# Loading and multiplying the gate and up matrices of two neighbouring experts together, in 64-row groups

## The chip, the cores and the metric

The kernel runs on one NeuronCore of a Trainium2 chip. The metric is the device time of one execution in microseconds (us); lower is better. All tensors are float32.

## The reference, cut to what matters

Two layers are computed on 256 tokens of width 1024. Each layer has an attention mixer (MLA, block-sparse and dilated heads in parallel) and then a mixture of experts. The change touches the experts alone:

```python
# 64 experts in 8 groups, top-2 inside the best group, D_MODEL 1024, D_EXPERT 256
def one_block(args):
    toks, e = args
    xb = x_pad[toks]                                  # the tokens of expert e
    hb = jax.nn.silu(xb @ w1[e]) * (xb @ w3[e])       # gate and up: 1024 -> 256 each
    return hb @ w2[e]                                 # down: 256 -> 1024
x = layer_norm(ALPHA * x + ffn, ln2_g[l], ln2_b[l])
```

Every expert has tokens or may have them, so all 64 experts' weights are read in each layer: w1 and w3 of 1 MB each and w2 of 1 MB per expert, 192 MB per layer.

## The kernel before, in words

**Tiling.** The program is written out by hand for each engine, with semaphores. Of each layer, an attention part comes first (lines 793 to 919 on TensorE), then the experts. These are taken four at a time: a batch is 4 experts (`NB`) with 32 token slots each (`BLK`), so 128 slots, and there are 16 batches per layer (`BATCHES`). The loop bound `m` is read from `iters` and is 14 here. Batches 0 and 1 are written out, 2 to 13 run in a loop of two batches (`Fori(2, m, 2)`, one on the even and one on the odd buffers), 14 is written out, and 15 has a form of its own (`last_batch`, lines 1174 to 1218) in which weights come in smaller parts.

**One batch on TensorE** (`batch`, lines 1154 to 1172), in this order: `up_gate` for the 4 experts (line 1030): for each expert 8 chunks c of the contraction, each a product of a 128-row, 32-column stationary piece of `xg` with 512 moving columns (gate and up side by side), the chunks spread over the four 32-column groups of the array. The partial sums of the four column groups are copied to `partial` (DVE for experts 0 and 2, line 1626; ACT for 1 and 3, line 1897 through the helper at 1724) and added by `fold` (1065). `turn_gated` (1071) transposes the slot weights. `gather(b + 1)` (1015) makes the next batch's `xg` in banks 2 and 3: 8 chunks of 128 slots, each summed over two token tiles, with a column piece of `x` stationary and the 0/1 matrix `chosen` moving. DVE (1569) and ACT (1880) copy the two banks to `xg`, 4 chunks of 128x128 each, and apply the norm's scale and shift, which stand per partition in `g_cols`. `turn_hidden_pairs` (1086) turns the hidden values; DVE copies them (1646). TensorE waits for both halves of the next `xg` (lines 1167, 1168), since `down_pairs` (1100) writes banks 2 and 3. DVE (1662) and ACT copy its result, and `add_all` (1112) adds it to the output banks.

**down_pairs already works on pairs.** The w2 matrices of two experts come in one transfer with 16 KB per partition (`load_w2_pairs`, line 397): partitions 0 to 63 hold expert 2q, 64 to 127 hold expert 2q+1. A product takes 64 rows and 32 columns of the array. Expert k writes column group k and reads row half k % 2, so each column group sees one row half only:

```python
q, z = k // 2, k % 2
rows = slice(64 * z, 64 * z + 64)
last = mm(bank[2 + h][BLK * k:BLK * (k + 1), :], hT_pair[rows, c, BLK * q:BLK * (q + 1)],
          w2_pairs[parity][q][rows, c, 512 * h:512 * h + 512], start=c == 0, stop=c == 3)
```

**Transfers.** All weights go through SyncE's queue. In a batch, w1 and w3 of expert k are two transfers of 1 MB (8 KB per partition, line 389), issued when the batch two earlier has used the slot (`part_psum`, line 486), and the two w2 pairs (2 MB each) when its down products are done (`y2_psum`). There are two sets of buffers, even and odd. The loads of batches 0 and 1 are issued during attention.

Of the kernel before, what the change touches and what calls it, by code (L numbers as in the profile page):

```python
# [19 lines left out]
P = 128  # L20
NT = SEQ // P
# [7 lines left out]
DC = DM // P  # L29
NE, NG, EPG, FE, TOP_K = 64, 8, 8, 256, 2  # L30
BLK = 32
# [49 lines left out]
def program(nc, a, consts, const_at, out):  # L81
# [12 lines left out]
    w2 = a["moe_w2"].rearrange("l e (p c) d -> (l e) p (c d)", c=2)  # L94
    w2_pair = a["moe_w2"].rearrange("l (g z) (p c) d -> (l g) (z p) (c d)", z=2, c=4)
# [4 lines left out]
    with ctx:  # L100
# [6 lines left out]
        small = sb("small", 416)  # L107
# [17 lines left out]

        w2_pairs = [pair_views(w2_even), pair_views(w2_mem)]
        w13_slots = [w13_views(w13_even), w13_views(w13_mem)]
# [67 lines left out]
        xg = part(DC * P).rearrange("p (c s) -> p c s", c=DC)  # L195
# [53 lines left out]
        n2_cols = small[:, 400:416].rearrange("p (v c) -> p v c", v=2)  # L249
        shift = small[:, 76:78]  # L250
# [20 lines left out]
        cols_in = Signal("norm_columns_in", 6 * 16)  # L271
# [95 lines left out]
        def _(sp):  # L367
# [3 lines left out]
            for l in range(DEPTH):  # L371
# [109 lines left out]
                def load_first(j, back, e, parity, last=False, by_matrix=False):  # L481
                    for k in range(NB):
# [3 lines left out]
                        sp.wait_ge(part_psum.sem, (b0 + j) * NB + (part_psum.start + k + 1 - back))  # L486
                        plain(sp)
                        load_w13(e, k, parity, last, (1,) if by_matrix and k == 0 else (0, 1))

                def load_batch(j, back, e, parity, last=False):  # L490
                    load_first(j, back, e, parity, last)
                    sp.wait_ge(y2_psum.sem, (b0 + j) + (y2_psum.start + 1 - back // NB))
                    plain(sp)
# [36 lines left out]
        def _(pool):  # L530
# [5 lines left out]
            for l in range(DEPTH):  # L536
# [9 lines left out]
                after(pool, l, cols_in, 96)  # L546
# [39 lines left out]
        def _(pe):  # L586
# [15 lines left out]
            xc = x.rearrange("p t (c d) -> p t c d", c=DC)  # L602
            slots_of = [ident.rearrange("p (q z s) -> p z q s", q=2, z=2)[:, z] for z in range(2)]
            for l in range(DEPTH):
# [415 lines left out]
                def up_gate(j, parity, k):  # L1020
                    b = b0 + (j + parity)
                    pe.wait_ge(w13_in[parity][k].sem, (b0 + j) * 16 + (32 - 16 * l * (parity and k == NB - 1)))
# [11 lines left out]
                def first_up_gate():  # L1034
                    pe.wait_ge(w13_in[0][0].sem, b0 * 16 + 32)
# [94 lines left out]
                def first_batch():  # L1130
                    first_up_gate()
                    up_gate(0, 0, 1)
                    after(pe, l, seed_act, 1)
                    seed_rows(0)
                    up_gate(0, 0, 2)
                    up_gate(0, 0, 3)
# [17 lines left out]
                def batch(j, parity, pairs=True):  # L1154
                    b = b0 + (j + parity)
                    pe.wait_ge(xg_dve.sem, b + 1)
                    for k in range(NB):
                        up_gate(j, parity, k)
# [815 lines left out]
```

## Time and profile before

| what | us |
|---|---|
| median of 3 runs | 1159.87 (1158.64 to 1160.63) |
| the profiled execution's own time | 1159.31 |
| its span, first to last instruction | 1157.5 |
| TensorE busy | 1040.3 (90%) |
| VectorE (DVE) busy | 384.4 (33%) |
| ScalarE (ACT) busy | 236.8 (20%) |
| HBM read | 439.07 MB, 380 GB/s over the span |
| mean granted TensorE clock | 0.991 |

Times in the profile count from the first instruction. TensorE's busy time is the time in which at least one product runs; products on different groups of the array overlap, so the mean duration of one product is longer than its share of the busy time. "Idle before, releaser" is the time an engine stood still ahead of an instruction, and what ended that.

### The profile page before, as it was taken

Reading aid. Unit: us, or ns where it says so; the run is one execution under the profiler, and the core shown is the slowest. Engines: PE = TensorE matmul, PEld = TensorE weight load, DVE = VectorE, ACT = ScalarE, POOL = GpSimd, SP = SyncE. Lnnn points to the kernel's source line nnn. Section 1 sums busy time; section 2 is a strip of 40 time slices with the busy share of each in tenths; the row PEclk is TensorE's granted clock in tenths of the full one; section 3 lists DMA queues with packets and bytes.
Section 4 is the critical chain, followed back from the end, with each engine's and each line's share of the span. In section 5 each row is a group of like instructions: output and inputs, shape, how many; then the busy total and the mean of one; then the engine's idle time right before and its main releaser. Section 6 shows DMA issues by size and latency. Waiting matters only on the chain.

```text
span 1157.5 us, 19198 instructions
## 1 busy us (share of the span) xinstructions
PE 1040.3 (90%) x7546; PEld 519.1 (45%) x7546; DVE 384.4 (33%) x1093; ACT 236.8 (20%) x587; POOL 18.7 (2%) x36
## 2 busy tenths in 40 slices
PE   9999988888989988887999999989988989888888
PEld 6665753334433333333456657434433333333333
DVE  4875532222222222121268656222222222221213
ACT  1245321111111111111122543111111111111111
POOL 0010000000000000000000100000000000000000
PEclk9999999999999999999999999999999999998999
DMA  9957699999999999999995676999999999999997
GB/s 309 348 222 291 258 390 416 422 420 423 423 424 422 424 423 423 423 422 422 386 323 217 267 298 273 412 410 421 422 422 422 424 422 423 421 423 423 422 422 275
DMA packets 86029, 440.75 MB, mean 381 GB/s; under 512 B 17376, under 2 KB 36960, under 8 KB 44512
## 3 DMA queue, kind: packets, MB, share of 16 engines
q1 hardware_dynamic: 85696, 439.50, 93.9%
q8 instruction: 29, 0.48, 0.2%
q0 software_dynamic: 144, 0.58, 0.1%
q14 instruction: 16, 0.13, 0.0%
q10 hardware_dynamic: 144, 0.07, 0.0%
HBM read 439.07 MB, written 1.05 MB: 380 GB/s over the span
## 4 chain that ended last, share of the span: by engine, by line
PE 54%; SPq 32%; DMA 4%; DVE 4%; issue 3%; ACT 2%; POOL 0%; DVEq 0%; POOLq 0%
SPq L389 24%; PE bank L1030 9%; PE bank L662 9%; PE bank L1100 7%; SPq L399 7%; PE bank L1112 5%; PE bank L1015 5%; PE bank L788 4%; DMA w_even<-in_moe_w 3%; PE bank L1106 2%; PE bank L652 2%; DMA w_odd<-in_moe_w 2%; PE bank L1065 1%; PE bank L922 1%; SPq L514 1%
## 5 line engine op out<-in xcount | busy, mean ns | idle before, releaser
L1724 ACT ACTIVATE moe<-bank 128x512 f32<-128x512 f32 (+2 forms) x164 | 84.1, 523 | 596.6 <-PE bank L1030 337.5
L1112 PE MATMUL bank<-moe 128*128 128x512 f32 (+1 forms) x264 | 119.3, 593 | 23.7 <-DVE moe L1662 22.5
L1626 DVE COPY moe<-bank 128x512 f32<-128x512 f32 x64 | 44.2, 691 | 250.0 <-PE bank L1030 245.4
L1030 PE MATMUL bank<-w_even,moe 128*32 128x512 f32 x992 | 115.5, 610 | 11.5 <-DMA w_even<-in_moe_w 11.5
L1100 PE MATMUL bank<-w_even,moe 64*32 64x512 f32 x896 | 99.0, 590 | 18.3 <-ACT moe L1880 16.7
L1015 PE MATMUL bank<-moe,x 128*128 128x128 f32 x960 | 113.3, 277 | 1.9 <-DVE moe L1662 1.9
L1030 PE MATMUL bank<-w_odd,moe 128*32 128x512 f32 x992 | 110.6, 594 | 4.0 <-DMA w_odd<-in_moe_w 4.0
L1015 PEld LDWEIGHTS bank<-moe,x 128*128 128x128 f32 x960 | 110.6, 193 | 2.2 <-issue 2.2
L1100 PE MATMUL bank<-w_odd,moe 64*32 64x512 f32 x768 | 84.8, 590 | 15.7 <-DVE moe L1646 9.0
L1662 DVE COPY moe<-bank 128x512 f32<-128x512 f32 x32 | 22.1, 691 | 219.6 <-PE bank L1100 194.5
L1112 PEld LDWEIGHTS bank<-moe 128*128 128x128 f32 x264 | 47.2, 189 | 96.1 <-DVE moe L1662 49.0
L662 PE MATMUL bank<-w_even,w_odd 128*128 128x384 f32 x240 | 81.3, 489 | 0.0
L1030 PEld LDWEIGHTS bank<-w_even,moe 128*32 128x32 f32 x992 | 30.9, 111 | 88.6 <-issue 67.6
L1030 PEld LDWEIGHTS bank<-w_odd,moe 128*32 128x32 f32 x992 | 30.1, 110 | 82.2 <-issue 69.3
L1100 PEld LDWEIGHTS bank<-w_even,moe 64*32 64x32 f32 x896 | 32.8, 107 | 73.7 <-issue 73.7
L1880 ACT ACTIVATE moe<-bank,small 128x128 f32<-128x128 f32 x120 | 45.1, 456 | 98.5 <-PE bank L1015 98.5
L662 PEld LDWEIGHTS bank<-w_even,w_odd 128*128 128x128 f32 x240 | 44.5, 190 | 29.1 <-issue 2.0
L1065 PE MATMUL bank<-moe,constants 128*32 128x512 f32 (+1 forms) x272 | 35.4, 589 | 23.8 <-ACT moe L1724 23.8
L1100 PEld LDWEIGHTS bank<-w_odd,moe 64*32 64x32 f32 x768 | 28.1, 107 | 63.2 <-issue 63.2
L1634 DVE SCALAR_TENSOR_TENSOR moe<-moe,bank 128x256 f32<-128x256 f32 x32 | 13.5, 421 | 126.8 <-ACT moe L1900 126.8
L1569 DVE TENSOR_SCALAR moe<-bank,small 128x128 f32<-128x128 f32 x120 | 41.0, 403 | 24.6 <-PE bank L1015 24.6
L788 PE MATMUL bank<-w_odd 128*128 128x512 f32 x96 | 44.9, 602 | 0.1
(195 smaller groups left out, 904.7 us busy)
## 6 DMA issues: line engine op xcount, KB each, us to landing
w_odd<-in_moe_w SPq DMA_DIRECT2D x140, 1024.0 KB, 30.3
w_even<-in_moe_w SPq DMA_DIRECT2D x136, 1024.0 KB, 28.6
w_even<-in_moe_w SPq DMA_DIRECT2D x28, 2048.0 KB, 29.1
w_odd<-in_moe_w SPq DMA_DIRECT2D x24, 2048.0 KB, 30.3
w_even<-in_w_in SPq DMA_DIRECT2D x24, 768.0 KB, 11.6
w_odd<-in_w_out SPq DMA_DIRECT2D x4, 2048.0 KB, 13.4
w_odd<-in_moe_w SPq DMA_DIRECT2D x8, 512.0 KB, 12.3
w_even<-in_w_in SPq DMA_DIRECT2D x4, 416.0 KB, 6.8
```

Of the source, the lines that this page charges most:

```text
L389: sp.dma_start(w13_slots[parity][k][:, m, :, :].rearrange("p c f -> p (c f)"), (w1, w3)[m][l * NE + e * NB + k]).then_inc(sig.sem, 16)
L399: sp.dma_start(w2_pairs[parity][q].rearrange("p c d -> p (c d)"), w2_pair[l * (NE // 2) + e * (NB // 2) + q]).then_inc(w2_in[parity][2 * q ...
L662: last = mm(to[:, 0:GW], rows[:, c, :], weights[:, c, :], start=fresh and c == 0, stop=c == DC // 2 - 1, skip_group_check=True)
L788: last = mm(mix_bank[t][h][:, :], oT[:, c, t * P:(t + 1) * P], w_out_half[h][:, c, :], start=c == 0, stop=c == DC - 1, skip_group_check=True)
L1015: last = mm(bank[2 + c // 4][:, c % 4 * P:(c % 4 + 1) * P], xc[:, t, c, :], chosen[:, t, :], start=t == 0, stop=t == 1)
L1030: last = mm(bank[k % 2][BLK * q:BLK * (q + 1), :], xg[:, c, BLK * k:BLK * (k + 1)], w[:, :, c, :], start=c < 4, stop=c >= 4)
L1065: last = mm(to[BLK * k:BLK * (k + 1), 0:cols.stop - cols.start], const("fold"), partial[:, k, cols], start=True, stop=True)
L1100: last = mm(bank[2 + h][BLK * k:BLK * (k + 1), :], hT_pair[rows, c, BLK * q:BLK * (q + 1)], w2_pairs[parity][q][rows, c, 512 * h:512 * h + ...
L1112: return mm(Y[t][h][:, lo - 512 * h:hi - 512 * h], scatter[:, t * P:(t + 1) * P], y_rows[:, lo:hi], start=False, stop=True, skip_group_che ...
L1626: nc.vector.tensor_copy(partial[:, k, :], bank[2 if first and k == 0 else 0][:, :]).then_inc(part_dve.sem, 1)
L1724: return fn(dst, src, ACT.Copy)
L1880: last = fn(xg[:, c, :], bank[3][:, (c - 4) * P:(c - 3) * P], ACT.Identity, scale=g_cols[:, 0, c:c + 1], bias=g_cols[:, 1, c:c + 1])
```

## The change

Batches 3 to 14 of each layer take w1 and w3 in pairs of experts. Batches 0, 1, 2 and 15 keep the old form. Per batch, SyncE issues 4 transfers of 2 MB (16 KB per partition) in place of 8 of 1 MB, and both of a pair wait until both experts of the slot pair are used. `up_gate_pair` computes with 64-row, 32-column pieces: 16 chunks per expert, experts 2q and 2q+1 alternating on row halves 0 and 1, each in its own bank (0 to 3), chunk c on column group c % 4. `gather_pairs` makes the matching `xg`: for each of 16 chunks it writes 64 slots of expert 2q to partitions 0 to 63 and 64 of expert 2q+1 to 64 to 127. DVE and ACT copy 8 pieces of 128x64 each with `pair_cols`, which four more small transfers per layer bring. The even loop now runs from 4 on, and batches 2 and 3 are written out ahead of it.

```diff
+    w1_pair = a["moe_w1"].rearrange("l (g z) (p c) f -> (l g) (z p) (c f)", z=2, c=2 * DC)
+    w3_pair = a["moe_w3"].rearrange("l (g z) (p c) f -> (l g) (z p) (c f)", z=2, c=2 * DC)
...
+        xg_pair = xg_mem.rearrange("p (c s) -> p c s", c=2 * DC)
...
+                    for z in range(2):
+                        sp.dma_start(pair_cols[64 * z:64 * z + 64, v, :], a[name].rearrange("l (p c) -> l p c", c=2 * DC)[l]
+                                     ).then_inc(cols_in.sem, 16)
...
-                        sp.wait_ge(part_psum.sem, (b0 + j) * NB + (part_psum.start + k + 1 - back))
+                        done = 2 * (k // 2) + 2 if last else k + 1
+                        sp.wait_ge(part_psum.sem, (b0 + j) * NB + (part_psum.start + done - back))
...
+                def load_pairs(j, back, e, parity):
+                    for q in range(NB // 2):
+                        sp.wait_ge(part_psum.sem, (b0 + j) * NB + (part_psum.start + 2 * q + 2 - back))
+                        plain(sp)
+                        for m_ in range(2):
+                            sp.dma_start(w13_pairs[parity][q][:, m_, :, :].rearrange("p c f -> p (c f)"),
+                                         (w1_pair, w3_pair)[m_][l * (NE // 2) + e * (NB // 2) + q]
+                                         ).then_inc(w13_in[parity][2 * q + m_].sem, 16)
...
+            xc_pair = x.rearrange("p t (c d h) -> p t h c d", c=DC, h=2)
+            chosen_pair = chosen.rearrange("p t (q z s) -> p t z q s", q=2, z=2)
...
+                def gather_pairs(b):
+
+                    pe.wait_ge(chosen_ok.sem, b + 1)
+                    plain(pe)
+                    for h in range(2):
+                        for c in range(DC):
+                            for t in range(NT):
+                                for z in range(2):
+                                    last = mm(bank[2 + h][64 * z:64 * z + 64, 64 * c:64 * c + 64], xc_pair[:, t, h, c, :],
+                                              chosen_pair[:, t, z], start=t == 0, stop=t == 1)
+                        last.then_inc(gathered[h].sem, 1)
+
+                def up_gate_pair(j, parity, q):
...
+                    for c in range(2 * DC):
...
+                        i = c % 4
+                        for z in range(2):
+                            rows = slice(64 * z, 64 * z + 64)
+                            last = mm(bank[2 * q + z][BLK * i:BLK * (i + 1), :], xg_pair[rows, c, BLK * q:BLK * (q + 1)],
+                                      w[rows, :, c, :], start=c < 4, stop=c >= 2 * DC - 4)
+                            if c == 2 * DC - 1:
+                                last.then_inc(part_psum.sem, 1)
...
-                with pe.Fori(2, m, 2) as j:
+                batch(0, 1, 32 + 32 * l, pairs=False, next_pairs=False)
+                batch(2, 0, 48 + 32 * l)
+                batch(2, 1)
+                with pe.Fori(4, m, 2) as j:
                     batch(j, 0)
                     batch(j, 1)
-                batch(m, 0)
+                batch(m, 0, next_pairs=False)
...
+                    if pairs:
+                        for c in range(DC):
+                            last = ts(xg_pair[:, c, :], bank[2][:, 64 * c:64 * c + 64], pair_cols[:, 0, c:c + 1],
+                                      pair_cols[:, 1, c:c + 1], ALU.mult, ALU.add)
+                        last.then_inc(xg_dve.sem, 1)
+                        return
...
-                        nc.vector.tensor_copy(partial[:, k, :], bank[2 if first and k == 0 else 0][:, :]).then_inc(part_dve.sem, 1)
+                        source = bank[k if w13_pairs else 2 if first and k == 0 else 0]
+                        nc.vector.tensor_copy(partial[:, k, :], source[:, :]).then_inc(part_dve.sem, 1)
...
+                    if pairs:
+                        for c in range(DC):
+                            last = fn(xg_pair[:, DC + c, :], bank[3][:, 64 * c:64 * c + 64], ACT.Identity,
+                                      scale=pair_cols[:, 0, DC + c:DC + c + 1], bias=pair_cols[:, 1, DC + c:DC + c + 1])
+                        last.then_inc(xg_act.sem, 1)
+                        return
```

The third and fourth partial sums of a batch are now read from banks 2 and 3, so the waits of `up_gate` for a free bank (line 1025) fall away in these batches. The waits on `w13_in` count one increment per transfer of a pair.

## Rows read from the trace of the kernel before

**Rows 1.** The page: GB/s in 40 equal slices of the span.

```profile
GB/s 309 348 222 291 258 390 416 422 420 423 423 424 422 424 423 423 423 422 422 386 323 217 267 298 273 412 410 421 422 422 422 424 422 423 421 423 423 422 422 275
```

**Rows 2.** The page: the chain that ended last, by engine (SPq is SyncE's queue).

```profile
PE 54%; SPq 32%; DMA 4%; DVE 4%; issue 3%; ACT 2%; POOL 0%; DVEq 0%; POOLq 0%
```

**Rows 3.** Timeline of TensorE, batch 8 of layer 0: start us, us, what, count [idle before].

```profile
357.85 7.07 PE L1030 MATMUL bank<-w_even,moe 128*32 128x512 f32 x64
...
367.00 3.74 PE L1015 MATMUL bank<-moe,x 128*128 128x128 f32 x32
370.67 0.69 PE L1086 MATMUL bank<-constants,moe 128*64 128x64 f32 x16
372.63 7.07 PE L1100 MATMUL bank<-w_even,moe 64*32 64x512 f32 x64 [1.28 <-ACT moe L1880]
```

**Rows 4.** Timeline of TensorE: first up_gate products of batches 3, 11, 15, both layers.

```profile
226.84 3.64 PE L1030 MATMUL bank<-w_odd,moe 128*32 128x512 f32 x32
...
436.56 5.36 PE L1030 MATMUL bank<-w_odd,moe 128*32 128x512 f32 x48
...
553.58 5.40 PE L1030 MATMUL bank<-w_odd,moe 128*32 128x512 f32 x48
...
799.54 7.07 PE L1030 MATMUL bank<-w_odd,moe 128*32 128x512 f32 x64
...
1009.35 5.36 PE L1030 MATMUL bank<-w_odd,moe 128*32 128x512 f32 x48
...
1127.41 5.36 PE L1030 MATMUL bank<-w_odd,moe 128*32 128x512 f32 x48
```

**Rows 5.** Timeline of TensorE: stretches that ran at the lower clock, both layers.

```profile
472.68 3.49 PE L1030 MATMUL bank<-w_even,moe 128*32 128x512 f32 x16 [2.86 <-DMA w_even<-in_moe_w]
...
1045.31 2.69 PE L1030 MATMUL bank<-w_even,moe 128*32 128x512 f32 x16 [2.87 <-DMA w_even<-in_moe_w]
...
1051.13 4.71 PE L1015 MATMUL bank<-moe,x 128*128 128x128 f32 x32
...
1104.82 3.36 PE L1030 MATMUL bank<-w_even,moe 128*32 128x512 f32 x16 [2.87 <-DMA w_even<-in_moe_w]
```

**Rows 6.** DMA view: 295 to 300 us (16 KB packets), then 305 to 319 us (8 KB).

```profile
DMA packets 147, 2.15 MB, mean 429 GB/s; under 512 B 16, under 2 KB 16, under 8 KB 16
...
DMA packets 812, 5.89 MB, mean 421 GB/s; under 512 B 93, under 2 KB 93, under 8 KB 93
```

**Rows 7.** Timeline of SyncE's queue, layer 0: w1 and w3 of batches 2 and 3 issued.

```profile
149.72 8.99 SPq L389 DMA_DIRECT2D w_even<-in_moe_w  x8
...
179.88 5.96 SPq L389 DMA_DIRECT2D w_odd<-in_moe_w  x8
```

**Rows 8.** Timeline of TensorE: four 32-row groups at once, each with its bank.

```profile
66.31 0.71 PE L735 MATMUL bank<-w_odd 32*128 32x256 f32 x8
```

**Rows 9.** Timeline of TensorE, 370.70 to 371.10 us: 14 of the 16 products.

```profile
370.67 0.63 PE L1086 MATMUL bank<-constants,moe 128*64 128x64 f32 x14
```

**Rows 10.** Groups of ACT by form, whole span: busy us, mean ns | idle before.

```profile
L1724 ACT ACTIVATE moe<-bank 128x512 f32<-128x512 f32 x92 | 54.9, 597 | 556.4 <-PE bank L1030 337.5 <-PE bank L1100 195.2 <-PE bank L947 15.8
L1880 ACT ACTIVATE moe<-bank,small 128x128 f32<-128x128 f32 x120 | 45.1, 456 | 98.5 <-PE bank L1015 98.5
...
L1724 ACT ACTIVATE moe<-bank 128x256 f32<-128x256 f32 x40 | 15.3, 383 | 26.5 <-PE bank L1106 20.0 <-PE bank L1059 3.4 <-PE bank L1071 3.2
...
L1852 ACT ACTIVATE moe<-moe 128x64 f32<-128x64 f32 x4 | 1.0, 257 | 10.9 <-DVE moe L1506 10.9
```

**Rows 11.** Timelines of ACT and DVE, batch 8 of layer 0: the copies of the next xg.

```profile
370.78 1.50 ACT L1880 ACTIVATE moe<-bank,small 128x128 f32<-128x128 f32 x4 [3.19 <-PE bank L1015]
...
368.99 1.37 DVE L1569 TENSOR_SCALAR moe<-bank,small 128x128 f32<-128x128 f32 x4 [0.67 <-PE bank L1015]
371.40 0.42 DVE L1646 COPY moe<-bank 128x256 f32<-128x256 f32 x1 [1.04 <-PE bank L1086]
```

**Rows 12.** DMA view, 250 to 540 us: the queue that carries instructions.

```profile
q14 instruction: 2, 0.02, 0.0%
```

More of the change, by code:

```diff
@@ L124, in pair_views, with w13_pair_views @@
             return [mem[:, q * 2 * W2:(q + 1) * 2 * W2].rearrange("p (c d) -> p c d", c=4) for q in range(NB // 2)]
+        def w13_pair_views(mem):
+            return [mem[:, q * 2 * W13:(q + 1) * 2 * W13].rearrange("p (m c f) -> p m c f", m=2, c=2 * DC)
+                    for q in range(NB // 2)]
         w2_pairs = [pair_views(w2_even), pair_views(w2_mem)]
+        w13_pairs = [w13_pair_views(w13_even), w13_pair_views(w13_mem)]
         w13_slots = [w13_views(w13_even), w13_views(w13_mem)]
@@ L545, in _ @@
                 after(pool, l, router_in, 32)
-                after(pool, l, cols_in, 96)
+                after(pool, l, cols_in, 160)
                 after(pool, l, comb, 8)
@@ L1152, in first_batch, with batch @@
                     add_all()
-                def batch(j, parity, pairs=True):
+                def batch(j, parity, seen=None, pairs=True, next_pairs=True):
                     b = b0 + (j + parity)
                     pe.wait_ge(xg_dve.sem, b + 1)
-                    for k in range(NB):
-                        up_gate(j, parity, k)
+                    if seen is None:
+                        for q in range(NB // 2):
+                            up_gate_pair(j, parity, q)
+                    else:
+                        for k in range(NB):
+                            up_gate(j, parity, k, seen)
                     pe.wait_ge(part_dve.sem, b * 2 + 2)
@@ L1163, in batch @@
                     turn_gated(bank[1])
-                    gather(b + 1)
+                    (gather_pairs if next_pairs else gather)(b + 1)
                     pe.wait_ge(scT_sb.sem, b + 1)
@@ L1601, in _ @@
                 weigh_scores(1)
-                after(v, l, cols_in, 96)
+                after(v, l, cols_in, 160)
                 def scale_first(c):
@@ L1613, in _, with batch @@
                 m, b0 = start_batches(v, base, l)
-                def batch(j, last_of_all, e_next, first=False, pairs=False):
+                def batch(j, last_of_all, e_next, first=False, pairs=False, w13_pairs=False, next_pairs=False):
                     b = b0 + j
@@ L1893, in _, with copy_partial @@
                 scale_first(7).then_inc(xg_act.sem, 1)
-                def copy_partial(b, k):
+                def copy_partial(b, k, source=bank[1]):
                     act.wait_ge(part_psum.sem, b * NB + (part_psum.start + k + 1))
-                    copy(partial[:, k, :], bank[k % 2][:, :]).then_inc(part_act.sem, 1)
+                    copy(partial[:, k, :], source[:, :]).then_inc(part_act.sem, 1)
                 def squash():
@@ L1904, in copy_scatter, with batch @@
                     copy(scatter, source[:, 0:SEQ]).then_inc(scT_sb.sem, 1)
-                def batch(j, first=False):
+                def batch(j, first=False, w13_pairs=False, next_pairs=False):
                     b = b0 + j
                     copy_partial(b, 1)
-                    copy_partial(b, 3)
+                    copy_partial(b, 3, bank[3 if w13_pairs else 1])
                     act.wait_ge(gu_psum.sem, b + 1)
@@ L1940, in _ @@
                 batch(0, first=True)
-                with act.Fori(1, m) as j:
-                    batch(j)
-                batch(m)
+                batch(1)
+                batch(2, next_pairs=True)
+                with act.Fori(3, m) as j:
+                    batch(j, w13_pairs=True, next_pairs=True)
+                batch(m, w13_pairs=True)
                 last_batch(m + 1)
```

56 lines of the change are left out of this document (35 added, 21 removed).

## The prediction, made before the changed kernel was built or run

> **What bounds the kernel now.** I read the GB/s line of the page first. In the two long expert stages it stands at 420 to 424 in slice after slice [rows 1]: the transfers never pause there, so each layer's experts last as long as their weights take to arrive. The chain that ended last says so too: a third of it is SyncE's queue, which only issues loads [rows 2]. The third view is TensorE's timeline, and it is the one that decides here, since TensorE is close behind. The reader is to see in it the order of one batch [rows 3] and the pace of batches [rows 4]. From the first up_gate product of batch 3 to that of batch 11, eight batches take 436.56 - 226.84 = 209.72 us, 26.2 us each, and in layer 1 1009.35 - 799.54 = 209.81, the same. A batch's weights are 12.58 MB, at 421 GB/s [rows 6] 29.9 us. So TensorE is the faster by 3.7 us a batch; it begins with a lead of the transfers (batches 0 and 1 were loaded during attention), and has used it up at about batch 11. From there it waits for data: batches 11 to 15 start over 117.02 us in layer 0 and 118.06 in layer 1, against 4 x 26.2 = 104.9.
>
> **The slack this leaves.** It is 117.02 - 104.9 = 12.1 us in layer 0 and 13.2 in layer 1. Not all of it is waiting. In some stretches TensorE ran at the lower clock [rows 5], and that time stays. Forty-eight up_gate products take 5.36 us and 64 take 7.07 [rows 3, 4], so 0.107 each and 0.2 to drain, and 16 should take 1.9; they took 3.49 in layer 0 (1.6 lost), and 2.69 and 3.36 in layer 1 (2.3 lost). Layer 1's gather took 4.71 in place of 3.74 (1.0 lost), and from the end of the products before it to its start were 3.1 us in place of 2.1 (another 1.0). So the real slack is 10.5 us in layer 0 and 8.9 in layer 1. **A batch of TensorE's work may grow by that over 12, 0.7 to 0.9 us, before the change costs time**, since 12 batches of each layer (3 to 14) are changed and 12 gathers (in batches 2 to 13).
>
> **Part 1, the transfers.** The trace has both sizes side by side: 16 KB packets (w2) at 429 GB/s, 8 KB packets at 421 [rows 6]. The 8.39 MB of w1 and w3 per batch take 19.93 us at the one and 19.56 at the other: 0.37 us saved, times 12 is 4.4 us per layer. Against it stands the wait for both experts of a pair. It matters once per layer: the loads for batch 2 start at 149.7 and need 29.9 us, those for batch 3 are issued at 179.9 [rows 7], so the queue is just empty there, and the new wait comes a quarter of up_gate later, 7.07/4 = 1.8 us [rows 3]. Later on the queue is over a batch deep and the coarser wait is covered by it. Bounds: 0 to 1.8 us lost, I take 1.8, as the rows leave no cover. The stream of transfers ends 2.6 us earlier per layer. Fewer issues on SyncE, four small loads more per layer during attention, and waits of GpSimd and ACT for them: nothing, covered by the attention part, where SyncE is ahead.
>
> **Part 2, up_gate on TensorE.** 32 products of 128 rows become 64 of 64 rows. If both row halves of a column group work at once, the time is the same 7.07 us; if not, it doubles. The trace has row groups running together over the same columns, each with its own bank: eight instructions of 32 rows and 256 columns in 0.71 us [rows 8], where one instruction streams 256 columns in half the 0.43 us that 512 take (64 on four column groups in 7.07 less 0.2), so one after another they would be 1.7. It has column groups running together [rows 3]. It has no case of both. The down products don't show it, since there each column group sees one row half. Bounds 0 and +7.07; I take 0, the nearest row being that of the row groups. The page TensorEngine Tiling (Array Packing) of the Trainium skill, section Tiling Modes, lists 64x32 as eight tiles that work independently, and its Restrictions and Gotchas ask for different banks for different row tiles. The change gives each row half its own bank, so by that page too the term is 0; no row here shows all eight.
>
> **Part 3, the gather on TensorE.** 16 products (32 instructions) of 128 stationary columns, 3.74 us [rows 3], become 64 products (128 instructions) of 64 stationary and 64 moving columns. turn_hidden_pairs is the same form: 16 instructions in 0.69 us, 14 in 0.63 [rows 3, 9], so 0.03 each. 127 x 0.03 plus 0.24 for the last is 4.05 us: +0.3. Bounds: 0, as the columns in all are the same; and 0.69/16 = 0.043 each, 5.5 us, +1.8.
>
> **Part 4, the copies of xg, the part that weighs most.** ACT can start only when the second half of the gather is done, and down waits for it: after 0.69 us of turn_hidden TensorE stands for 1.28 us for L1880 [rows 3]. The four copies take 1.50 us [rows 11], the last of them 0.456 [rows 10], so 0.348 from start to start. Eight copies of half the width follow. From 256 to 512 columns a copy grows from 383 to 597 ns [rows 10], 0.84 ns a column, so 64 columns fewer save 54 ns: 0.294 from start to start and 0.40 for the last, 7 x 0.294 + 0.40 = 2.46 us: +0.96. Bounds: 64-column activations without the per-partition columns take 257 ns, eight of them 2.06, +0.55; and if the interval doesn't shrink at all, 2.89, +1.39. Nothing covers it: TensorE waits already. DVE's eight copies grow too (1.37 us for four), by the same reckoning to 2.2, but they start half a gather earlier, at 369.0, and would end at 371.2, ahead of the next copy at 371.4 [rows 11]: nothing, with 0.2 us of cover. If it is gone, DVE's copy of the hidden values is late next, and still ends ahead of ACT.
>
> **Part 5, the rest.** The waits for free banks fall away; they ended nothing. The last two partial sums end together, and DVE's 0.69 us copy is the last; add_all waits 0.8 us behind such a copy as fold does behind ACT's: nothing.
>
> **The sum.** TensorE's batch grows by 0.3 + 0.96 = 1.26 us, over 12 batches 15.1 us. That is more than the slack: 15.1 - 10.5 = 4.6 us in layer 0 and 15.1 - 8.9 = 6.2 in layer 1, together 10.8. TensorE is then the bound from end to end, and the 2.6 us per layer of the transfers come to nothing. The profiled execution took 1159.31 us, which gives 1170.1; the median of the runs is 0.56 higher. With a little back in the last batches, where data will lie ready, I say 1170.
>
> **Rivals.** A, the forecast: TensorE slower than the stream by a little. For it speaks that TensorE already waits for ACT at that place. With the upper bounds (1.8 + 1.39 = 3.2 us a batch, 38 per layer) it reaches 1217, with both terms a third up 1181.
> B, faster: TensorE's growth stays under (10.5 - 2.6)/12 = 0.66 us a batch, and the stream stays the bound. Price: -2.6 us per layer, 1154.7, and 1151 if the pair wait costs nothing. For it: the lower bounds add to 0.55. Against it: the copies carry two per-partition columns each, and the 64-column row has none.
> C, the row halves don't run together: +7.07 us a batch more, 8.3 x 12 = 100 per layer less the slack, 181 us in all, 1340. For it: no row shows eight pieces at once. Against it: rows 8.
> D, the loop's code no longer stays in the engine. TensorE's part of a loop pass grows from 194 x 2 products' instructions to 354 x 2, each with its weight load, 776 to 1416. Between 250 and 540 us only two small instruction packets came [rows 12], so the old loop ran from memory on the engine. If the new one doesn't, each of the four returns per layer waits for a fetch, behind data: a 16 KB packet takes 0.6 us (131 of them in 5 us on 16 engines [rows 6], the 16 small ones left out), and with four ahead of it that is 3 us, an estimate: 8 x 3 = 24 us, 1194. The Trainium skill, page Runtime: NRT & Kernel Launch, section Instruction fetch mechanics, gives TensorE room for 2048 instructions, and says a branch to code outside waits; by its size the new loop fits and the term is 0, but it also says that only two lines of 256 are held, by which the old loop would have fetched on each pass, and rows 12 show that it didn't.
>
> **How the numbers follow.** A 0.66, B 0.20, C 0.07, D 0.07. The time is A's, 1170. The range leaves out C and the upper ends of A and D, and reaches down to B: 1154 to 1187. A measurement of this kernel can tell some 0.2% (2.3 us) from no change. Faster by more: B less its margin, 0.18. Within: the edge of A and B, 0.10. Slower: 0.72.
>
> **What would show it.** Right: in the timeline the idle time ahead of the down products grows from 1.28 to some 2.2 us and is put down to ACT; its eight copies take 2.5 us; gather_pairs takes 4.0; up_gate_pair's 128 instructions take 7.1; batches are 27.5 us apart from 3 to 15 with no waits for w_even or w_odd, and GB/s falls below 420 in the last slices of each stage. Wrong: waits for data in batches 12 to 15 (B), 14 us for up_gate_pair (C), pauses at every second batch with 16 KB instruction packets (D).

## The result, and the profile after

The changed kernel takes **1183.38 us** (median of 4 runs, 1180.47 to 1185.21) where the kernel before took 1159.26 beside it (1156.78 to 1160.63): the ratio is 1.0211, with a 95% interval from 1.0196 to 1.0226. It is slower by 24.1 us. The forecast had the direction and the place right, but it said 10.8 us more, 1170, and the growth is more than twice that. The profiled execution took 1184.07 us, its span is 1182.2. All medians are of executions at the usual clock; one of filled_wait's four executions ran at a mean clock of 0.752, took 1460.11 us and is left out.

The page after, two lines: GB/s in 40 slices of the span, and the chain that ended last by engine.

```profile
GB/s 307 329 225 286 290 399 393 427 426 426 428 428 429 428 429 427 429 429 413 296 240 178 269 298 270 413 424 428 425 427 427 428 429 429 427 429 428 426 398 86
...
PE 86%; DVE 7%; issue 4%; ACT 3%; POOL 0%; DVEq 0%; POOLq 0%
```

Two things changed against [rows 1, 2]. The transfers run at 425 to 429 GB/s in place of 420 to 424, and in the last slices of a stage they have little left to do (413 and 296 near the end of layer 0, 398 and 86 at the end of layer 1, where it was 422 and 275). SyncE's queue, a third of the chain before, has left it: 86% is TensorE. The bound has moved from the stream to TensorE in both layers.

TensorE's timeline after, one batch of layer 0 from its up_gate product to the next batch's (start us, us, what, count, idle before and what ended it). L1074 is up_gate_pair, L1124 fold, L1130 turn_gated, L1056 gather_pairs, L1145 turn_hidden_pairs, L1159 down_pairs, L1171 add_rows.

```profile
373.96 7.10 PE L1074 MATMUL bank<-w_even,moe 64*32 64x512 f32 x128
381.93 1.07 PE L1124 MATMUL bank<-moe,constants 128*32 128x512 f32 x8 [0.87 <-DVE moe L1698]
382.93 0.44 PE L1130 MATMUL bank<-constants,moe 128*128 128x128 f32 x2
383.30 4.06 PE L1056 MATMUL bank<-moe,x 128*64 128x64 f32 x128
387.19 0.64 PE L1145 MATMUL bank<-constants,moe 128*64 128x64 f32 x16
390.23 7.07 PE L1159 MATMUL bank<-w_even,moe 64*32 64x512 f32 x64 [2.40 <-ACT moe L1954]
398.10 3.70 PE L1171 MATMUL bank<-moe 128*128 128x512 f32 x8 [0.80 <-DVE moe L1734]
401.74 7.10 PE L1074 MATMUL bank<-w_odd,moe 64*32 64x512 f32 x128
```

Beside [rows 3]: up_gate_pair's 128 instructions take 7.10 us where 64 took 7.07; the gather takes 4.06 where it took 3.74; and the idle time ahead of the down products is 2.40 us where it was 1.28. This batch lasts 401.74 - 373.96 = 27.78 us and the odd one before it 27.65, against 26.2. No up_gate product of batches 2 to 15 waits for data any more.

The timelines of ACT and DVE after, in the batch before it: the copies of the next xg, and DVE's copy of the hidden values.

```profile
359.78 2.47 ACT L1954 ACTIVATE moe<-bank,small 128x64 f32<-128x64 f32 x8 [3.64 <-PE bank L1056]
...
357.86 2.11 DVE L1635 TENSOR_SCALAR moe<-bank,small 128x64 f32<-128x64 f32 x8 [0.97 <-PE bank L1056]
360.24 0.42 DVE L1718 COPY moe<-bank 128x256 f32<-128x256 f32 x1 [0.28 <-PE bank L1145]
```

ACT's eight copies take 2.47 us where four took 1.50 [rows 11]; DVE's end at 359.97, 0.28 us before their queue's next work is ready.

TensorE's timeline after, the products of layer 0 that ran long, and a pause in one gather. Layer 1 has four more of the same kind (at 801.54, 887.84, 917.04 and 1029.59) and one more pause (1.26 us, ended at 884.85).

```profile
217.28 8.77 PE L1159 MATMUL bank<-w_even,moe 64*32 64x512 f32 x64 [2.41 <-ACT moe L1954]
...
300.45 0.46 PE L1056 MATMUL bank<-moe,x 128*64 128x64 f32 x9 [1.40 <-issue]
...
303.64 8.75 PE L1159 MATMUL bank<-w_odd,moe 64*32 64x512 f32 x64 [2.27 <-issue]
...
333.11 8.77 PE L1159 MATMUL bank<-w_even,moe 64*32 64x512 f32 x64 [2.41 <-ACT moe L1954]
...
445.69 8.77 PE L1159 MATMUL bank<-w_even,moe 64*32 64x512 f32 x64 [2.42 <-ACT moe L1954]
```

The same 64 down products take 8.77 us here and 7.07 elsewhere, 1.7 us lost each time (1.4 at 887.84). TensorE's totals from 218.40 to 221.60 us show why: the last three numbers are the granted clock as a share of full speed, the share of the DMA engines and GB/s, and 0.50 is the lower of the clock's two levels, 1.2 in place of 2.4 GHz.

```profile
218.40:221.60 3.20, 3.20 (x20) 1.06 (x16) 0.00 (x0) 0.00 (x0) 0.00 (x0) 0.50 1.01 425
```

There are eight such stretches, each in the down products behind the long wait for ACT; before there were three places [rows 5], in other products. Two of the eight (303.64 and 887.84) also stand behind the pause in the gather. A stretch in batch 0 of one layer or both, which every kernel here has (before at 162.58 and 735.13 us), is left out of all counts.

**Where the 24.1 us come from.** The spans differ by 1182.2 - 1157.5 = 24.7 us. A pair of batches lasts 401.74 - 346.31 = 55.43, so one 27.7, which is 1.49 more than before; in 2 x 12 batches that is 35.7. The gap that TensorE had before between its pace and the stream's, 12.1 + 13.2 us with all that was lost in it to the lower clock, swallows 25.3 of it: 10.4 stay. Eight stretches at the lower clock add 13.3 (seven of 1.7 and one of 1.4), the two pauses 2.7. Two small things come back: waits for data in layer 0's last batch (1.0), and the stretch at the lower clock in batch 0 of layer 1, which the kernel before had at 735.13 us and this one has not (1.7). The sum is 23.7 of the 24.7 by which the spans differ.

### The profile page after: what moved, and what is told of

It is laid out like the page before. It is cut to its first block, busy times and chain, and to the rows that moved or that the text cites. A ratio compares the mean times of both kernels' runs of the same rounds, so it can differ in the third digit from the quotient of the medians.

```text
span 1182.2 us, 26727 instructions
## 1 busy us (share of the span) xinstructions
PE 1051.9 (89%) x11386; PEld 537.4 (45%) x11386; DVE 403.6 (34%) x1189; ACT 260.1 (22%) x683; POOL 18.7 (2%) x36
## 4 chain that ended last, share of the span: by engine, by line
PE 86%; DVE 7%; issue 4%; ACT 3%; POOL 0%; DVEq 0%; POOLq 0%
PE bank L1159 17%; PE bank L1074 14%; PE bank L1171 10%; PE bank L690 8%; PE bank L1056 8%; PE bank L1089 4%; PE bank L816 4%; PE bank L1124 3%; ACT moe L1954 2%; PE bank L680 2%; PE bank L1165 2%; DVE moe L1734 2%; PE bank L1043 2%; DVE moe L1698 1%; PE bank L950 1%
## 5 line engine op out<-in xcount | busy, mean ns | idle before, releaser
L1171 PE MATMUL bank<-moe 128*128 128x512 f32 (+1 forms) x264 | 119.3, 593 | 24.4 <-DVE moe L1734 23.3
L1159 PE MATMUL bank<-w_even,moe 64*32 64x512 f32 x896 | 109.2, 640 | 31.5 <-ACT moe L1954 29.0
L1159 PE MATMUL bank<-w_odd,moe 64*32 64x512 f32 x768 | 87.9, 608 | 27.1 <-issue 27.1
L1056 PE MATMUL bank<-moe,x 128*64 128x64 f32 x3072 | 98.1, 224 | 2.7 <-issue 2.7
L1056 PEld LDWEIGHTS bank<-moe,x 128*64 128x64 f32 x3072 | 94.5, 139 | 7.0 <-issue 7.0
L1171 PEld LDWEIGHTS bank<-moe 128*128 128x128 f32 x264 | 47.3, 190 | 96.9 <-DVE moe L1734 49.7
L1074 PE MATMUL bank<-w_odd,moe 64*32 64x512 f32 x1536 | 85.2, 591 | 0.0
L1074 PE MATMUL bank<-w_even,moe 64*32 64x512 f32 x1536 | 85.2, 591 | 0.0
L1954 ACT ACTIVATE moe<-bank,small 128x64 f32<-128x64 f32 x192 | 59.3, 415 | 90.2 <-PE bank L1056 90.2
L1159 PEld LDWEIGHTS bank<-w_even,moe 64*32 64x32 f32 x896 | 35.5, 114 | 94.4 <-issue 94.4
L1159 PEld LDWEIGHTS bank<-w_odd,moe 64*32 64x32 f32 x768 | 28.3, 109 | 77.5 <-issue 77.5
L1635 DVE TENSOR_SCALAR moe<-bank,small 128x64 f32<-128x64 f32 x192 | 50.6, 336 | 22.7 <-PE bank L1056 22.7
L1124 PE MATMUL bank<-moe,constants 128*32 128x512 f32 (+1 forms) x272 | 34.5, 576 | 25.4 <-DVE moe L1698 21.0
L1074 PEld LDWEIGHTS bank<-w_odd,moe 64*32 64x32 f32 x1536 | 28.0, 107 | 55.3 <-issue 55.3
L1074 PEld LDWEIGHTS bank<-w_even,moe 64*32 64x32 f32 x1536 | 28.0, 107 | 55.3 <-issue 55.3
L1797 ACT ACTIVATE w_odd<-bank 128x256 f32<-128x256 f32 (+3 forms) x60 | 27.7, 468 | 85.0 <-PE bank L651 27.4
```

The costliest lines, as they stand in the source:

```text
L1056: last = mm(bank[2 + h][64 * z:64 * z + 64, 64 * c:64 * c + 64], xc_pair[:, t, h, c, :], chosen_pair[:, t, z], start=t == 0, stop=t == 1)
L1074: last = mm(bank[2 * q + z][BLK * i:BLK * (i + 1), :], xg_pair[rows, c, BLK * q:BLK * (q + 1)], w[rows, :, c, :], start=c < 4, stop=c >= 2 ...
L1124: last = mm(to[BLK * k:BLK * (k + 1), 0:cols.stop - cols.start], const("fold"), partial[:, k, cols], start=True, stop=True)
L1171: return mm(Y[t][h][:, lo - 512 * h:hi - 512 * h], scatter[:, t * P:(t + 1) * P], y_rows[:, lo:hi], start=False, stop=True, skip_group_che ...
L1635: last = ts(xg_pair[:, c, :], bank[2][:, 64 * c:64 * c + 64], pair_cols[:, 0, c:c + 1], pair_cols[:, 1, c:c + 1], ALU.mult, ALU.add)
L1797: return fn(dst, src, ACT.Copy)
```

## The experiments

The forecast's terms were all in place, and the time was 13 us further. The theory to test (**T**): ACT's copies, on which the down products wait, cost the growth of the batch, and the longer standstill of TensorE brings the stretches at the lower clock. Its rivals: the pace of the transfers or the pair wait costs it (**R1**), the gather's shape does (**R2**), and the stretches come from TensorE's share of work or from chance, not from the wait (**R3**).

### late_wait: ACT's xg is waited for one half later

Nothing in the down products reads xg. The wait for ACT stands there because the second half of them writes bank 3, from which ACT copies; the first half writes bank 2, which DVE has emptied long before. So the wait can move by one half: out of batch() and into the loop over the halves in down_pairs.

```diff
                     for h in range(2):
+                        if h:
+                            pe.wait_ge(xg_act.sem, b0 + (j + parity) + 2)
+                            plain(pe)
...
-                    pe.wait_ge(xg_act.sem, b + 2)
+                    if not pairs:
+                        pe.wait_ge(xg_act.sem, b + 2)
```

> Edit: in the changed kernel, TensorE waits for ACT's half of the next xg only ahead of the second half of the down products (the ones that overwrite bank 3), not ahead of the first. Theory 1 (the eight narrow ACT copies on TensorE's path are what costs): the 2.4 us standstill ahead of down falls to that of DVE's copy of the hidden values, about 0.9 us, a batch shrinks from 27.7 to about 26.2 us, the stream of transfers is the bound again and its 16 KB packets show: about 1154 us, 5 below the kernel before. Theory 2 (the new products themselves, 128 instructions each for gather and up_gate, and their fetches hold TensorE back): the batch keeps most of its growth and the time stays above 1170.

Measured: 1154.87 us (1152.88 to 1158.08), ratio to the kernel before 0.9969 [0.9958, 0.9979]: faster than both kernels. TensorE's timeline of late_wait, an odd and an even batch of layer 0, and one wait for data later on:

```profile
348.71 7.07 PE L1162 MATMUL bank<-w_odd,moe 64*32 64x512 f32 x64 [0.62 <-DVE moe L1722]
...
360.22 7.10 PE L1074 MATMUL bank<-w_even,moe 64*32 64x512 f32 x128
...
374.81 7.07 PE L1162 MATMUL bank<-w_even,moe 64*32 64x512 f32 x64 [0.72 <-DVE moe L1722]
...
500.17 5.19 PE L1074 MATMUL bank<-w_odd,moe 64*32 64x512 f32 x64 [3.04 <-issue]
```

The down products now wait 0.72 us for DVE's copy of the hidden values, the batch is 386.32 - 360.22 = 26.1 us, and TensorE waits for data again. With one wait moved, 28.5 us went. The gather's shape and the pair wait are still in this kernel, so R1 has no part in the loss. R2 has a small one: the gather and its start take 0.31 us more per batch, 7.4 us in 24 batches, which this kernel's slack hides and the changed kernel's does not.

### before_late_wait: the same edit in the old kernel

> Edit: the same later wait for ACT's half of xg, in the kernel before. Theory 1: the kernel before is bound by the stream of transfers, so TensorE's saving of some 0.5 us a batch only lengthens its waits for data: 1159 us, within 1 us of before. If the kernel before were bound by TensorE, it would gain 10 us or more.

Measured: 1159.51 us, ratio 1.0007 [0.9994, 1.0020]. There the stream was the bound, and a faster TensorE only waits longer for it. The gain of late_wait is thus not the moved wait's own: it is the transfers' larger packets, which show once TensorE is out of the way.

### late_wait_8k: the pair transfers cut into 8 KB per partition again

Each load of a pair's matrix is issued as two of half the size, the first with a semaphore of its own, for which up_gate_pair waits too; everything else is late_wait.

```diff
-    sp.dma_start(w13_pairs[parity][q][:, m_, :, :].rearrange("p c f -> p (c f)"),
-                 (w1_pair, w3_pair)[m_][l * (NE // 2) + e * (NB // 2) + q]
-                 ).then_inc(w13_in[parity][2 * q + m_].sem, 16)
+    for u in range(2):
+        sig = (w13_half, w13_in)[u][parity][2 * q + m_]
+        sp.dma_start(w13_pairs[parity][q][:, m_, DC * u:DC * u + DC, :].rearrange("p c f -> p (c f)"),
+                     (w1_pair, w3_pair)[m_][l * (NE // 2) + e * (NB // 2) + q][:, DC * FE * u:DC * FE * (u + 1)]
+                     ).then_inc(sig.sem, 16)
```

> Edit: the kernel with the later wait (late_wait), in which each 2 MB transfer of a w1 or w3 pair is cut in two of 1 MB with 8 KB per partition; products and order stay. Theory: late_wait (1154.9 us) is bound by the stream of transfers and is faster than before by its 16 KB packets. By 421 GB/s against 429 for these 8.39 MB a batch, 0.37 us a batch or 8.8 us in all are lost: about 1163 us. Rival (the size of packets does not matter, late_wait gains by something on TensorE): within 1.5 us of late_wait.

Measured: 1164.09 us, ratio 1.0056 [1.0038, 1.0073]. The DMA view from 305 to 319 us, late_wait first:

```profile
DMA packets 415, 6.03 MB, mean 431 GB/s; under 512 B 47, under 2 KB 47, under 8 KB 47
```

and the same stretch of late_wait_8k:

```profile
DMA packets 806, 5.89 MB, mean 421 GB/s; under 512 B 91, under 2 KB 91, under 8 KB 91
```

The packet's size alone is worth 1164.09 - 1154.87 = 9.2 us, against 8.8 (twice 4.4) in Part 1. It also shows what the rest of the change costs the stream: with packets of the old size it is some 6 us slower than the kernel before beside it (1158.18 us). A pair wait at batch 3 is part of it. From 176 to 184 us of layer 0 the queue moved 398 GB/s before, 339 in late_wait_8k and 313 in the changed kernel, which is (398 - 339)/421 x 8 = 1.1 us for the one and 1.6 for the other (1.3 by the busy shares, 0.98 and 0.82). The other 3 to 4 us were not traced further.

### plain_copies: ACT's copies without scale and shift

The copies stay where they are, eight of 64 columns, but read no per-partition columns, so the kernel leaves the norm's scale and shift out of half of xg. `copy` also asks ACT for the function Copy where it was Identity.

```diff
-    last = fn(xg_pair[:, DC + c, :], bank[3][:, 64 * c:64 * c + 64], ACT.Identity,
-              scale=pair_cols[:, 0, DC + c:DC + c + 1], bias=pair_cols[:, 1, DC + c:DC + c + 1])
+    last = copy(xg_pair[:, DC + c, :], bank[3][:, 64 * c:64 * c + 64])
```

> Edit: in the changed kernel, ACT's eight narrow copies leave out the scale and shift columns (the norm's scale and shift are left out of half of xg, so the experts' inputs change). Theory 1: such a copy takes about 0.11 us from start to start in place of 0.29, the eight end 1.3 us earlier, TensorE's standstill falls from 2.4 to about 1.1 us, and the time to between 1154 and 1160. Theory 2 (the products hold TensorE back): it stays above 1170.

Measured: 1154.87 us, ratio 0.9973 [0.9962, 0.9984]. ACT's timeline of plain_copies, then TensorE's:

```profile
374.52 1.04 ACT L1797 ACTIVATE moe<-bank 128x64 f32<-128x64 f32 x8 [3.63 <-PE bank L1056]
```

```profile
375.91 7.07 PE L1159 MATMUL bank<-w_even,moe 64*32 64x512 f32 x64 [0.98 <-ACT moe L1797]
```

The eight copies take 1.04 us in place of 2.47, the wait 0.98 in place of 2.40, and the 28.5 us are gone again, with no wait moved. Two different edits, each of which takes 1.4 us or more out of that one standstill, give the same time, since in both the stream is the bound again: T's first half holds.

### before_narrow: the narrow copies in the old kernel

```diff
-    for c in range(4, DC):
-        last = fn(xg[:, c, :], bank[3][:, (c - 4) * P:(c - 3) * P], ACT.Identity,
...
+    for i in range(2 * DC // 2):
+        c, lo = 4 + i // 2, 64 * (i % 2)
+        last = fn(xg[:, c, lo:lo + 64], bank[3][:, 64 * i:64 * i + 64], ACT.Identity,
...
```

> Edit: in the kernel before, ACT's four copies of the next xg (128x128) become eight of 128x64 with the same scale and shift columns; nothing else. Theory: this is the changed kernel's main term alone. 0.97 us longer on TensorE's path in each of 13 batches per layer (1 to 14 but the first), 12.6 us a layer against a slack of 10.5 and 8.9 us: 2 and 4 us over, and up to 5 stretches more at the lower clock, 1.7 us each, as the standstill before down is as long as in the changed kernel: 1165 to 1174. Rival (the copies matter little, the 128-instruction products do): 1158 to 1160.

Measured: 1164.34 us (1160.49 to 1167.58), ratio 1.0048 [1.0029, 1.0067], just under the lower edge of what was expected. TensorE's timeline of before_narrow in batch 8 of layer 0 (L1071 turns, L1015 gathers, L1100 is down), and ACT's:

```profile
374.65 0.44 PE L1071 MATMUL bank<-constants,moe 128*128 128x128 f32 x2
374.93 3.74 PE L1015 MATMUL bank<-moe,x 128*128 128x128 f32 x32
...
381.52 2.78 PE L1100 MATMUL bank<-w_even,moe 64*32 64x512 f32 x24 [2.24 <-ACT moe L1881]
```

```profile
378.70 2.47 ACT L1881 ACTIVATE moe<-bank,small 128x64 f32<-128x64 f32 x8 [3.19 <-PE bank L1015]
```

Part 4's working is right to 0.01 us: 2.46 forecast for the eight copies, 2.47 measured, and the wait grows from 1.28 to 2.24, which is the 0.96. A batch lasts 27.2 us and no product waits for weights from batch 2 on, so TensorE is the bound here too. But there are only four stretches at the lower clock, one more than before, and two of them stand in batch 1, whose wait grew to 2.48 us. **A standstill of 2.2 us per batch does not bring the eight stretches by itself.** That was a miss for T's second half, and the next four runs go after it.

### filled_wait, filled_less, filled_third: work in the standstill

Dummy products into a free bank are issued ahead of the waits for xg, so that TensorE works while ACT copies. The diff is filled_wait's; filled_less has 6 and filled_third 2 in place of the 8.

```diff
+    if pairs and next_pairs:
+        keep_warm(8, bank[0])
     pe.wait_ge(xg_dve.sem, b + 2)
     pe.wait_ge(xg_act.sem, b + 2)
```

> Edit: in the changed kernel, eight dummy products (128x128, about 1.8 us) into a bank that is free run between turn_hidden_pairs and the wait for xg, so that TensorE does not stand still there; nothing else changes, the down products start no earlier. Theory 1 with the clock as a consequence of the standstill: the stretches at the lower clock, 8 in the expert stages of the changed kernel against 3 before, fall to about 3, and the time by 1.7 us for each that is gone: 1175. Rival (the stretches come from something else in the new products, or by chance): they stay about 8 and the time stays at 1183.

Measured: 1177.55 us, ratio 1.0151 [1.0126, 1.0177]. The eight dummies take 2.05 us behind a wait of 0.53 and run slightly past ACT's end, so the batch grows to 368.40 - 340.50 = 27.9. No stretch at the lower clock is left. The time is still 2.5 us above the 1175 expected: batches 2 to 4 of layer 1 hold three pauses, of 1.02, 1.39 and 0.88 us, in the gather or the turn behind it.

> Edit: the changed kernel with six dummy products in TensorE's wait for xg in place of the eight of filled_wait, so that they end before ACT does and the batch keeps the changed kernel's 27.7 us (eight made it 27.9). Theory: no stretches at the lower clock are left in the expert stages, and without the 0.2 us a batch that the eighth product cost the time is 1183.4 less 8 x 1.7 us: 1170 us. Rival (filled_wait was faster by chance): 1177 to 1183.

Measured: 1169.92 us (1168.34 to 1171.69), ratio 1.0094 [1.0078, 1.0111]. TensorE's timeline of filled_less, one batch of layer 0 (L622 are the dummies):

```profile
366.08 7.10 PE L1074 MATMUL bank<-w_even,moe 64*32 64x512 f32 x128
...
380.47 1.60 PE L622 MATMUL bank<-constants 128*128 128x128 f32 x12 [0.53 <-DVE moe L1720]
382.36 7.07 PE L1159 MATMUL bank<-w_even,moe 64*32 64x512 f32 x64 [0.29 <-ACT moe L1956]
390.24 3.70 PE L1171 MATMUL bank<-moe 128*128 128x512 f32 x8 [0.80 <-DVE moe L1736]
393.87 1.52 PE L1074 MATMUL bank<-w_odd,moe 64*32 64x512 f32 x24
```

This batch lasts 393.87 - 366.08 = 27.79 us, the changed kernel's own pace, since the dummies fit into the wait and ACT still ends it. Yet the kernel is 13.5 us faster. One stretch at the lower clock is left where the changed kernel has eight (7 x 1.7 = 11.9); its clock fell at 793.43 us, 1.4 us behind the end of the one pause that is left, of 1.38 us, and the changed kernel has two such pauses (2.7). Most of the 13.5 us is thus the lower clock's price, with the pace held.

> Edit: the changed kernel with two dummy products (four instructions, about 0.6 us) in TensorE's wait for xg, so that 1.2 us of the 2.4 us standstill are left ahead of down, about what the kernel before had. Theory (long standstills bring the lower clock): the stretches fall from 8 to 3 or fewer, as in the kernel before, and the time is 1170 to 1175 us. Rival (it takes a full wait to be rid of them): 5 or more stay, 1178 us or more.

Measured: 1174.52 us, ratio 1.0141 [1.0115, 1.0167]. With two dummies 1.18 us of standstill are left at a stretch, shorter than in the old kernel. The time is as expected, the count is not: five stretches, where at most three were expected. They stand at 270.06, 382.47, 850.57, 962.97 and 1075.36 us, 112.4 us or four batches apart within each layer (a third one in layer 0 would stand at 494.86 and did not come). TensorE's timeline of filled_third, two down products:

```profile
354.66 7.07 PE L1159 MATMUL bank<-w_odd,moe 64*32 64x512 f32 x64 [0.93 <-issue]
...
382.47 8.77 PE L1159 MATMUL bank<-w_even,moe 64*32 64x512 f32 x64 [1.18 <-ACT moe L1956]
```

### dummies_elsewhere: the same added work, the standstill kept

```diff
                     add_all()
+                    if pairs and next_pairs:
+                        keep_warm(6, bank[0])
```

> Edit: the changed kernel with the six dummy products of filled_less (1.5 us) after the batch's last product in place of in the wait. The standstill of 2.4 us stays and every one of 22 to 24 batches is about 1.5 us longer, 33 to 36 us in all, so 1183 + 35 = 1218 us with all 8 stretches at the lower clock. Theory (it is the standstill itself that brings the lower clock): about 8 stretches remain and the time is near 1218. Rival (it is the share of the batch in which TensorE works, wherever that work stands): the stretches go, and the time is near 1205.

Measured: 1242.57 us (1242.06 to 1243.89), ratio 1.0722 [1.0696, 1.0748], slower than either figure. TensorE's timeline of dummies_elsewhere, two batches that follow each other:

```profile
261.04 1.50 PE L622 MATMUL bank<-constants 128*128 128x128 f32 x12
...
278.76 8.77 PE L1159 MATMUL bank<-w_even,moe 64*32 64x512 f32 x64 [2.42 <-ACT moe L1956]
...
309.45 8.77 PE L1159 MATMUL bank<-w_odd,moe 64*32 64x512 f32 x64 [2.27 <-issue]
```

The stretch comes in **every** one of the twelve changed batches of a layer, the down products at 340.30, 370.99, 401.83 and so on included, and batches are 30.8 us apart. The working: 24 dummy groups, each of which makes its batch 1.34 us longer (32; two batches last 61.5 us, of which 3.4 are the lower clock's, against 55.4), and 16 stretches more than the changed kernel has (16 x 1.7 = 27) on 1183.4 make 1243. The clock granted over the two stages, with the down products' busy time, in dummies_elsewhere:

```profile
200.00:560.00 360.00, 100.86 (x732) 30.41 (x736) 0.94 1.00 417
780.00:1150.00 370.00, 96.55 (x704) 30.91 (x704) 0.95 0.99 416
```

and in filled_less, with the same number of dummies:

```profile
200.00:560.00 360.00, 91.92 (x832) 30.44 (x832) 1.00 1.01 427
780.00:1150.00 370.00, 92.88 (x832) 31.14 (x832) 1.00 1.00 422
```

(The fifth number is the clock as a share of full speed; the changed kernel has 0.98 in both.) Only one execution of each kernel was traced, but the mean clocks of the others agree with it: 0.985 to 0.988 in the changed kernel, 0.996 to 0.998 in filled_less, 0.997 to 1.000 in filled_wait, 0.989 to 0.991 in filled_third, 0.964 to 0.966 in dummies_elsewhere.

The same added work gives 1 stretch inside the standstill and one in every batch outside it, so the standstill is needed for most of the changed kernel's stretches. It is not enough to set their number, and neither is R3's first form, TensorE's share of work. By its three waits TensorE stands still for 4.1 us a batch in the changed kernel, 4.1 in dummies_elsewhere and 3.9 in before_narrow, and the stretches are 8, 24 and 4. That a stretch comes is not drawn at random either: filled_third has it four batches apart, dummies_elsewhere in every batch, with different distances between the standstills, and the changed kernel has gaps of 86, 29 and 113 us in layer 0 and of the same 86, 29 and 113 in layer 1. What sets the distance was not settled; nor was why before_narrow, with a standstill of 2.24 us in batches of some 27 us, got only four. The length of the batch and the new products' shapes differ between these kernels along with the standstill, and no run varied either of the two alone.

## Why the forecast missed, step by step

- **The slack this leaves, the failed step.** It took the lower clock's time of the old kernel as a fixed charge: "In some stretches TensorE ran at the lower clock, and that time stays." It did not stay. It went from 5.9 us (three places) to 13.3 (eight), 7.4 us of the 13 that were missing. The change lengthened the one standstill in each batch, which I had priced in Part 4 as idle time alone; a second price, the products behind it at half speed, stood in no term. filled_less shows that price: with the pace the same and the clock held up, the time falls by 13.5 us. That it falls to 1169.9, the forecast's own figure, is luck, as two misses cancel there: its batches are 1.45 us longer than before, not 1.26 (4.6 us more in all), and it loses 1.7 us to the lower clock where the forecast kept 5.9. Nor does the longer standstill alone bring the eight stretches (before_narrow has four); what else it takes stays open.
- **The sum, mis-sized.** The batch grew by 1.49 us and not 1.26, 5.5 us over 24 batches. By parts: the gather +0.22 (forecast 0.3); the gather's start behind turn_gated 0.37 us in place of 0.28, a term I had not; up_gate_pair 0.03 and fold, which waits for DVE's copy and not ACT's, 0.06 (forecast 0 for both); from turn_hidden to the down products 1.08 (forecast 0.96: the copies are right, ACT starts 0.12 us later behind the gather). On the 0.09 the Trainium skill has a rule, TensorEngine Tiling (Array Packing), section Key Properties: a change of tiling mode drains the engine. The gather is now tiled by 64 columns where turn_gated is not; the trace agrees in sign, at 0.09 us.
- **A lower bound that was none.** Part 4 took eight times 257 ns, 2.06 us, as the least for copies without the per-partition columns. But 257 ns is the length of one copy, not the distance from start to start; plain_copies has eight in 1.04 us. The forecast itself did not use it, rival B's lower end did.
- **The rest of the 13.** The pauses of 1.40 and 1.26 us in a gather had no term (2.7), and what came back in layer 0's last batch and in batch 0 of layer 1 takes as much off again. The first pause ends at 300.45 us, 1.35 us behind the landing of a 16 KB instruction packet, the second 1.38 us behind one (the DMA view of the changed kernel from 296 to 299 us has the first).

```profile
q8 instruction: 1, 0.02, 2.2%
```

Such pauses, twelve in seven of the kernels (0.64 to 1.81 us), all end 1.27 to 1.51 us behind such a landing, all in batches 2 to 5, before the loop has turned back once, and all in a changed gather or the turn behind it. The kernels with the old gather have none. That TensorE waits there for code it has not run yet fits all twelve; no run takes the packets away, so it is not shown.
- **Part 1, the transfers: right.** 428 against 421 GB/s, worth 9.2 us by late_wait against late_wait_8k (8.8 forecast); the pair wait 1.3 to 1.6 us where 1.8 was taken. It came to nothing in the changed kernel, as said, because TensorE is the bound.
- **Part 2: right.** Eight 64x32 pieces work at once: 128 instructions in 7.10 us, where one row half after the other would need 14. Rival C falls. By the Trainium skill (TensorEngine Tiling (Array Packing), section Tiling Modes) these are eight independent tiles, and the trace agrees with that.
- **DVE's cover: right.** 2.11 us for its eight copies (2.2 forecast) and 0.28 us of cover (0.2).
- **Rival B: false for this kernel, right for late_wait.** Growth under 0.66 us a batch was its condition and 1154.7 us its time. late_wait has a batch of 26.1 us and 1154.87, plain_copies 26.3 and the same time. The forecast had the point from which it decides; both edits went under it. The close time is partly luck: B gained 5.2 us on 1159.9, late_wait gains 3.5 on the 1158.37 beside it.
- **Rival D: false for the loop's returns.** The DMA view of the changed kernel from 320 to 540 us has one queue and no instruction packet:

```profile
DMA packets 6549, 94.19 MB, mean 428 GB/s; under 512 B 728, under 2 KB 728, under 8 KB 728
...
q1 hardware_dynamic: 6549, 94.19, 100.6%
```

The loop of some 1400 matrix instructions turned back four times per layer without a packet of code. What D feared may be at work in the first pass alone, in the pauses above, at 2.7 us and not 24. A 16 KB instruction packet took 1.07 us there, not the 0.6 that was estimated.

## What to carry to other kernels

Ask of every wait which later write or read needs it, and put it in front of that alone: here the wait for ACT guarded one bank of two, and moving it by half a stage turned a loss of 2.1% into a gain of 0.3%. When a change makes pieces half as wide, take the copies that follow them from start to start, as most of each is fixed (0.35 us became 0.29 for half the columns). And when a change lengthens a standstill of TensorE that recurs, charge for the clock too: look in the timeline for the same products that take 8.77 us in one batch and 7.07 in another, and keep a term with both ends for it, as these runs do not say how many such stretches come.

## What the runs showed of the hardware that was not expected

- A scale and a shift per partition cost ACT more than the columns do: eight 128x64 copies from PSUM take 2.47 us with them and 1.04 without, 0.29 and 0.11 from start to start. (The function changed too, from Identity to Copy; no run separates the two.)
- Stretches at the lower clock follow the standstills in a pattern by batches: none or one with the 2.4 us filled, four batches apart with 1.2 us left of it and batches of 28.1 us, in every batch with the standstill whole and batches of 30.8 us. Work added elsewhere did not help; it cost 59 us where its own time is 32.
- In late_wait one group of down products still ran at the lower clock (294.91 us, 8.77), behind a pause of 1.81 us in the gather (plain_copies shows the same at 295.32, behind 1.26). Its other two stretches stand in up_gate products behind waits for data of 3.04 and 3.17 us. In both kernels the long wait for ACT was gone, so the stretches are not tied to that wait; pauses of 0.64 and 0.98 us in layer 1 brought none. The gather of late_wait, in layer 0:

```profile
293.32 0.52 PE L1056 MATMUL bank<-moe,x 128*64 128x64 f32 x10 [1.81 <-issue]
```
